# Attention scores from rounded high and low parts instead of plain fp32 matmuls

## The chip, the core and the metric

One core of a Trainium2 chip. The time is that of the device for one launch, in microseconds (us), the median of the runs shown; smaller is better.

## The reference

One layer of a diffusion backbone on 128 context tokens and 1024 latent tokens, D_MODEL 1024: a SwiGLU half step, then attention beside a recurrent block (RG-LRU), then a second SwiGLU half step. The change touches the differential attention:

```python
s = jnp.einsum('bqhmd,bkhmd->bhmqk', qi, k) * scale      # 4 heads h, 2 maps m, d = 64
p = jax.nn.softmax(s, axis=-1)
pd = p[:, :, 0] - lam * p[:, :, 1]
return jnp.einsum('bhqk,bkhv->bqhv', pd.astype(v.dtype), v)
```

Context queries see the 128 context keys. Latent queries see 1024 latent keys, rotated by RoPE as the queries are, and 128 cached keys: 1152 in all. Everything is float32.

## The kernel before

Activations stand transposed, features on the partitions: x holds queries of head hd in tile hd (map 0 on partitions 0 to 63, map 1 on 64 to 127) and its keys in tile hd + 4. The FFN and the projections use products in two rounded parts: each operand is split into a high part (type fp32r, a rounding copy on ScalarE) and a low part (operand less high part, on VectorE), and three fp32r matmuls add high by high, high by low and low by high (`three`, lines 715 to 719). The attention scores don't: `scores` (line 1034) takes x and the cached keys kc as plain fp32, 64 rows per map, each map in its half of the array (`tile_position`). The trace has two records for each plain fp32 matmul and one for each fp32r matmul.

A unit u is one head (u // 9) and one tile of 128 queries (u % 9); unit 0 of a head is the context tile with 128 keys, the eight others are full units with 1152 keys. There are 36. PSUM has banks 0 to 2 for the scores of map 0, 3 to 5 for map 1, bank 6 for transposes and bank 7 for outputs, one copy of each. The four engines run written-out orders, one pass per u:

- TensorE: `scores(u)` (each map waits on e_done until its exponential of unit u-1 has been taken), then for unit u-2 three groups of three transposes through bank 6 (`group`), with the value products of unit u-3 between them (`values`, line 1061).
- VectorE (line 2323): the negated row maximum of each map (`maxima`), the copy of the middle group of transposes of unit u-2 (`p_copy`), the difference of the two maps of unit u-1 (three instructions), and the output of unit u-3.
- ScalarE (line 1593): copy of the first group of transposes, the exponentials of both maps with their sums, copy of the last group, and the squares of unit u-4's output.
- POOL: nothing until the norm of the outputs near the end. SP: all DMA.

Ahead of the loop, VectorE rotates the eight q and k tiles (`rope`), gates the recurrent block (`rg_gated`, line 2249) when xg is no longer needed, and computes lambda; SP then loads vc, ident, kc and dl over xg (N_ACST). ScalarE evicts the v products (`v_evac`), 15 ahead of the loop and three in it behind unit 1, where TensorE makes the last three v tiles (`v_last`). SP loads the first two tiles of w_out (lines 677 and 678) there; they are used at units 32 and later. When a head's last scores are done, SP reloads its two x tiles, which were spilled before.

## Time and profile before

| | |
|---|---|
| three runs | 2266.53, 2268.42, 2269.19 us; median 2268.42 |
| the profiled execution | span 2266.8 us from first to last instruction; the page gives no time around it |
| TensorE matmuls busy | 2191.9 us, 97% |
| VectorE, ScalarE, POOL busy | 1552.2 (68%), 815.4 (36%), 20.1 us (1%) |
| mean granted TensorE clock | 0.992 |

Busy time counts instructions that compute; a matmul's record is longer than the distance to the next, since they are pipelined, so the records of one group can add up to more than the time that they take. In the chain of what ended last each step goes back to what released it.

### The profile page before, as it was taken

What the parts mean: (1) busy time and instruction counts of PE and PEld (TensorE: products, weight loads), DVE (VectorE), ACT (ScalarE), POOL (GpSimd) and SP (SyncE); (2) the same over time, 40 slices, a digit from 0 to 9 for tenths busy, and PEclk for the clock granted to TensorE, in tenths of its full rate; (3) what the DMA queues carried; (4) which work ended last, traced back from release to release, by engine and by line L of the source; (5) the groups of instructions that cost most, each with busy time, mean ns of one, the idle gap of its engine ahead of it and who ended that gap; (6) DMA issues with size and microseconds to landing.
All of it is one profiled execution on the core that took longest, in us unless ns stands there. A gap on an engine that the chain in (4) does not pass through costs nothing.

```text
span 2266.8 us, 33980 instructions
## 1 busy us (share of the span) xinstructions
PE 2191.9 (97%) x13144; PEld 2105.5 (93%) x13144; DVE 1552.2 (68%) x2607; ACT 815.4 (36%) x1458; POOL 20.1 (1%) x31
## 2 busy tenths in 40 slices
PE   5999999999999999999999999999999999999997
PEld 4989999999999999889977779899999999999996
DVE  6977777778888776666668874686454556756556
ACT  5532222334111144654255662353232323421122
POOL 0000000000000000000000030000000000000000
PEclk9999999999999999999999999999999999999998
DMA  7433333344624304010110011132212123431312
GB/s 290 133 105 135 103 126 111 113 138 131 213 78 158 126 27 151 19 47 28 32 49 22 22 40 38 56 114 68 78 59 86 58 87 101 159 120 52 109 41 84
DMA packets 82292, 210.10 MB, mean 93 GB/s; under 512 B 9856, under 2 KB 36352, under 8 KB 82176
## 3 DMA queue, kind: packets, MB, share of 16 engines
q1 hardware_dynamic: 82176, 208.52, 27.4%
q8 instruction: 78, 1.28, 0.2%
q14 instruction: 38, 0.31, 0.0%
HBM read 172.56 MB, written 35.92 MB: 92 GB/s over the span
## 4 chain that ended last, share of the span: by engine, by line
PE 88%; DVE 7%; ACT 2%; DMA 1%; issue 1%; SPq 0%; DVEq 0%; ACTq 0%
PE ps L717 15%; PE ps L719 15%; PE ps L718 15%; PE ps L792 9%; PE ps L793 9%; PE ps L794 9%; PE ps L972 6%; PE ps L1043 4%; PE ps L1072 2%; PE ps L1058 1%; PE ps L954 1%; DVE sb_nmx L2286 1%; DVE sb_hL L1752 1%; DVE sb_tmp L1761 1%; PE ps L741 1%
## 5 line engine op out<-in xcount | busy, mean ns | idle before, releaser
L717 PE MATMUL ps<-sb_hH,sb_wH 128*128 128x384 f32 x1664 | 562.7, 338 | 10.2 <-DVE sb_hL L1752 4.7
L719 PE MATMUL ps<-sb_hH,sb_wL 128*128 128x384 f32 x1664 | 557.4, 335 | 0.0
L718 PE MATMUL ps<-sb_hL,sb_wH 128*128 128x384 f32 x1664 | 557.3, 335 | 0.0
L717 PEld LDWEIGHTS ps<-sb_hH,sb_wH 128*128 128x128 f32 x1664 | 313.4, 188 | 17.5 <-DVE sb_hL L1752 6.0
L718 PEld LDWEIGHTS ps<-sb_hL,sb_wH 128*128 128x128 f32 x1664 | 313.4, 188 | 1.1
L719 PEld LDWEIGHTS ps<-sb_hH,sb_wL 128*128 128x128 f32 x1664 | 313.4, 188 | 0.0
L2062 DVE SCALAR_TENSOR_TENSOR sb_x<-ps,sb_mod,sb_x 128x384 f32<-128x384 f32 (+2 forms) x384 | 186.2, 513 | 172.6 <-PE ps L719 167.2
L792 PE MATMUL ps<-sb_hH,sb_wH 128*128 128x384 f32 x704 | 236.1, 335 | 4.1 <-DVE sb_tmp L1922 3.9
L793 PE MATMUL ps<-sb_hL,sb_wH 128*128 128x384 f32 x704 | 235.9, 335 | 0.0
L794 PE MATMUL ps<-sb_hH,sb_wL 128*128 128x384 f32 x704 | 235.8, 335 | 0.0
L1226 ACT ACTIVATE sb_wH<-sb_wide 128x512 fp32r<-128x512 f32 x176 | 110.8, 633 | 229.1 <-DVE sb_wide L1806 224.0
L1215 ACT ACTIVATE sb_wH<-sb_raw 128x512 fp32r<-128x512 f32 x212 | 129.7, 627 | 172.3 <-PE ps L719 69.2
L1360 ACT ACTIVATE sb_wH<-sb_raw 128x512 fp32r<-128x512 f32 (+1 forms) x96 | 56.8, 596 | 371.0 <-PE ps L719 363.4
L1788 DVE TENSOR_TENSOR sb_wL<-sb_raw,sb_wH 128x512 fp32r<-128x512 f32 x212 | 139.7, 685 | 58.5 <-ACT sb_wH L1215 58.1
L794 PE MATMUL ps<-sb_r2H,sb_wL 128*128 128x384 f32 x528 | 176.4, 334 | 0.0
L792 PE MATMUL ps<-sb_r2H,sb_wH 128*128 128x384 f32 x528 | 176.4, 334 | 0.0
L793 PE MATMUL ps<-sb_r2L,sb_wH 128*128 128x384 f32 x528 | 176.4, 334 | 0.0
L792 PEld LDWEIGHTS ps<-sb_hH,sb_wH 128*128 128x128 f32 x704 | 132.7, 188 | 5.2 <-issue 5.2
L794 PEld LDWEIGHTS ps<-sb_hH,sb_wL 128*128 128x128 f32 x704 | 132.8, 189 | 0.0
L793 PEld LDWEIGHTS ps<-sb_hL,sb_wH 128*128 128x128 f32 x704 | 132.6, 188 | 0.0
L1812 DVE TENSOR_TENSOR sb_wL<-sb_wide,sb_wH 128x512 fp32r<-128x512 f32 x176 | 114.0, 684 | 2.4 <-DVE sb_rq L1863 1.1
L2286 DVE TENSOR_REDUCE sb_nmx<-ps 128x1 f32<-128x1152 f32 (+1 forms) x72 | 85.8, 1233 | 39.3 <-PE ps L1043 39.3
(244 smaller groups left out, 3789.3 us busy)
## 6 DMA issues: line engine op xcount, KB each, us to landing
sb_raw<-in_w_gate SPq DMA_DIRECT2D x56, 512.0 KB, 3.7
sb_raw<-in_w_up SPq DMA_DIRECT2D x56, 512.0 KB, 3.6
sb_raw<-in_w_mod SPq DMA_DIRECT2D x56, 512.0 KB, 3.5
hidden<-sb_tmp SPq DMA_DIRECT2D x132, 192.0 KB, 2.2
sb_hid_raw<-hidden SPq DMA_DIRECT2D x40, 576.0 KB, 6.5
sb_raw<-in_w_dn SPq DMA_DIRECT2D x80, 256.0 KB, 2.7
sb_stage<-in_w_mod SPq DMA_DIRECT2D x4, 2048.0 KB, 15.4
sb_raw<-in_w_in SPq DMA_DIRECT2D x16, 512.0 KB, 3.5
```

The lines of the kernel that those rows point to most:

```text
L717: pe.matmul(o, wH, xH, start=begin, stop=False)
L718: pe.matmul(o, wH, xL, start=False, stop=False)
L719: return pe.matmul(o, wL, xH, start=False, stop=end)
L792: pe.matmul(dst, wH[:, slot, at], opv(0, b, k), start=begin and k == 0, stop=False, skip_group_check=True)
L793: pe.matmul(dst, wH[:, slot, at], opv(1, b, k), start=False, stop=False, skip_group_check=True)
L794: m = pe.matmul(dst, wL[:, slot, at], opv(0, b, k), start=False, stop=k == 3, skip_group_check=True)
L972: m = pe.matmul(dst, (wiH, wiH, wiL)[part][:, f, at], hv((hH, hL, hH)[part], c, k), start=s == 0, stop=s == 3 * KT - 1)
L1215: act.activation(wH[:, o if slot is None else slot], raw_of(o, other), ACT.Copy).then_inc(one_hi[o], 1)
L1226: act.activation(wH[:, at], wide[:, 8 + at], ACT.Copy).then_inc(sum_hi, 1)
L1788: dve.tensor_tensor(wL[:, at], raw_of(o, other), wH[:, at].bitcast(F32), ALU.subtract).then_inc(one_lo[o], 1)
L1812: dve.tensor_tensor(wL[:, at], wide[:, 8 + at], wH[:, at].bitcast(F32), ALU.subtract).then_inc(sum_lo, 1)
L2062: m = dve.scalar_tensor_tensor(x[:, t, b:e], ps[:, DOWN_BANKS[n % 6], b - c * CH:e - c * CH], mod[:, gate + t, cond:cond + 1], x[:, t, b:e ...
```

## The change

Each full unit's scores are now sums of fp32r matmuls. Queries of head hd are rounded (high part) and stand twice on the 128 partitions, for each map by itself (`qstack`, `q_first`). Keys stand as high part on one half of the partitions and low part on the other (`kstack0` to `kstack2`, with the cached keys behind the latent ones). A 128-row matmul so gives high by high plus high by low at once, in three pieces of 384 keys, one for each bank. A third pass of 64 rows per map adds the low part of the queries times the high part of the keys (`low_scores`). Map 0 goes stacked then low, map 1 low then stacked, so that the low passes of both maps stand side by side. Context tiles stay as they were.

The low parts overwrite x in place (`qk_rest`). ScalarE rounds (`qk_high`) and VectorE subtracts (`qk_low`): head 0 ahead of the loop, the others at the units in SPLIT_AT. POOL issues the copies within SBUF that stack them, 12 for each head. The new buffers share space with raw, x, tmp, hL, wiH and xg. The w_out loads move behind the first head's last score.

```diff
@@ -60,9 +60,9 @@
 GROUP0 = [0] + [1 + 3 * t for t in range(9)]
 GROUPS = GROUP0[9]
 UNIT = LAT + 128
-PIECES = ((0, 0, 512), (0, 512, 1024), (1, 0, 512), (0, 1024, UNIT), (1, 512, 1024), (1, 1024, UNIT))
 MIX_ORDERS = ((0, 1, 2, 4, 5, 6, 7, 3), (4, 5, 6, 7, 0, 1, 2, 3), (4, 5, 6, 7, 0, 1, 2, 3))
 MIX_ORDER = MIX_ORDERS[1]
+SPLIT_AT = {1: (1, 0), 3: (1, 1), 5: (2, 0), 7: (2, 1), 11: (3, 0), 13: (3, 1)}
 LAM_INIT = 0.8 - 0.6 * math.exp(0.0)
 KEYS = T + 128
 GRID_W = 64
...
@@ -302,11 +320,27 @@
 
         ssf = ss[:].rearrange("p h t -> p (h t)")
 
-        psf = ps[:].rearrange("p b n -> p (b n)")
         o_first = raw[:, 2:4].rearrange("p a n -> p (a n)")
 
         def unit(u, m):
-            return psf[:, m * 1536:m * 1536 + KEY_TILES[u % QT] * P]
+            return ps[:, 3 * m:3 * m + 3, 0:CH] if u % QT else ps[:, 3 * m, 0:P]
+
+        def by_bank(row):
+
+            return row.rearrange("p (a n) -> p a n", a=3)
+
+        def queries(hd):
+
+            return qstack[:, hd - 1] if hd else q_first[:]
+
+        def keys_of(hd):
+
+            return (kstack0, kstack1, kstack2, kstack0)[hd]
+
+        def tile_hi(hd, is_k):
+
+            return 2 * hd + is_k + 1 + (hd > 0)
+
 
         def probs(u, m):
             return pr[:, u % 3, m, 0:KEY_TILES[u % QT] * P]
@@ -674,13 +708,13 @@
             sp.dma_start(out["v"], v[:, 0]).then_inc(outs, 16)
             sp.wait_ge(m_ev, 6 + 12 + QK * NC)
             sp.dma_start(out["k"].rearrange("h p t -> p h t"), x[:, 4:8, 0:CTX]).then_inc(outs, 16)
-            load_raw(0, used_wo[0], a["w_out"][0])
-            load_raw(1, used_wo[1], a["w_out"][1])
-
             sp.wait_ge(outs, 48)
             sp.wait_ge(spilled, 16 * KT)
             for hd in range(NH):
                 sp.wait_ge(s_ready, (hd + 1) * 2 * QT)
+                if hd == 0:
+                    load_raw(0, used_wo[0], a["w_out"][0])
+                    load_raw(1, used_wo[1], a["w_out"][1])
                 for k in (hd, hd + NH):
                     sp.dma_start(x[:, k], xd[k]).then_inc(xback, 16)
             with sp.Fori(0, 3) as i:
@@ -700,6 +734,41 @@
         @blk.gpsimd
         def _(pool):
 
+            top, bottom = slice(0, DH), slice(DH, P)
+
+            def stack_queries(hd):
+
+                pool.wait_ge(qk_hi, tile_hi(hd, 0))
+                if hd == 0:
+                    for s in range(2):
+                        pool.wait_ge(raw_used[s], used_wo[s] + 1)
+                elif hd == 1:
+                    pool.wait_ge(v_ready, 18)
+                for m, r in ((0, top), (1, bottom)):
+                    for to in (top, bottom):
+                        pool.dma_start(queries(hd)[to, m], qk_split[r]).then_inc(qk_moved, 16)
+
+            def stack_keys(hd):
+
+                pool.wait_ge(qk_hi, tile_hi(hd, 1))
+                if hd:
+                    pool.wait_ge(qk_in, 96 * hd)
+                if hd == 3:
+                    pool.wait_ge(s_ready, 2 * QT)
+                for m, r in ((0, top), (1, bottom)):
+                    pool.dma_start(keys_of(hd)[r, m, 0:LAT], qk_split[r]).then_inc(qk_moved, 16)
+                pool.wait_ge(qk_lo, tile_hi(hd, 1))
+                lows = qk_rest[:, hd + NH, CTX:T]
+                for m, r, to in ((0, top, bottom), (1, bottom, top)):
+                    pool.dma_start(keys_of(hd)[to, m, 0:LAT], lows[r]).then_inc(qk_in, 16)
+                pool.wait_ge(qk_lo, 3)
+                for m, r, to in ((0, top, bottom), (1, bottom, top)):
+                    pool.dma_start(keys_of(hd)[r, m, LAT:UNIT], kcH[r, hd]).then_inc(qk_in, 16)
+                    pool.dma_start(keys_of(hd)[to, m, LAT:UNIT], kcL[r, hd]).then_inc(qk_in, 16)
+
+            for hd in range(NH):
+                stack_queries(hd)
+                stack_keys(hd)
             pool.wait_ge(o_rec, 1)
             for c in range(NC):
                 for hd in range(NH - 1):
@@ -1031,19 +1100,50 @@
                     m = pe.transpose(ps[:, turn_bank(c, hd), k * P:(k + 1) * P], attended(hd, c * 3 + k), ident[:])
                 m.then_inc(ot_ready, 1)
 
-            def scores(u):
-
-                hd, q = u // QT, u % QT
-                for m, b, e in ((0, 0, P), (1, 0, P)) if q == 0 else PIECES:
-                    if b == 0 and 2 * u + m > 1:
+            def context_scores(u):
+
+                hd = u // QT
+                for m in range(2):
+                    if u:
                         pe.wait_ge(e_done, 2 * u + m - 1)
                     r = slice(m * DH, (m + 1) * DH)
-                    at = CTX if q else 0
-                    keys = kc[r, hd] if b == LAT else x[r, hd + NH, at + b:at + e]
-                    mm = pe.matmul(unit(u, m)[:, b:e], x[r, hd, q * P:(q + 1) * P], keys, start=True, stop=True,
-                                   tile_position=(m * DH, 0))
-                    if e == (UNIT if q else P):
-                        mm.then_inc(s_ready, 1)
+                    pe.matmul(unit(u, m), x[r, hd, 0:P], x[r, hd + NH, 0:P], start=True, stop=True,
+                              tile_position=(m * DH, 0)).then_inc(s_ready, 1)
+
+            def stacked_scores(u, m, begin):
+
+                hd, q = u // QT, u % QT
+                for p in range(3):
+                    mm = pe.matmul(ps[:, 3 * m + p, 0:CH], queries(hd)[:, m, (q - 1) * P:q * P],
+                                   keys_of(hd)[:, m, p * CH:(p + 1) * CH], start=begin, stop=not begin)
+                return mm
+
+            def low_scores(u, m, p, begin):
+
+                hd, q = u // QT, u % QT
+                r = slice(m * DH, (m + 1) * DH)
+                return pe.matmul(ps[:, 3 * m + p, 0:CH], qk_rest[r, hd, q * P:(q + 1) * P],
+                                 keys_of(hd)[r, m, p * CH:(p + 1) * CH], start=begin, stop=not begin,
+                                 tile_position=(m * DH, 0))
+
+            def scores(u):
+
+                hd, q = u // QT, u % QT
+                if q == 0:
+                    context_scores(u)
+                    return
+                if q == 1:
+                    pe.wait_ge(qk_lo, tile_hi(hd, 0))
+                    pe.wait_ge(qk_moved, 96 * hd + 96)
+                    pe.wait_ge(qk_in, 96 * hd + 96)
+                pe.wait_ge(e_done, 2 * u - 1)
+                stacked_scores(u, 0, True)
+                pe.wait_ge(e_done, 2 * u)
+                for p in range(3):
+                    mm = low_scores(u, 0, p, False)
+                    low_scores(u, 1, p, True)
+                mm.then_inc(s_ready, 1)
+                stacked_scores(u, 1, False).then_inc(s_ready, 1)
 
             def group(u, g):
 
@@ -1537,7 +1637,20 @@
                 later_evac(i)
                 if i % NC == NC - 1:
                     gelu_of(i // NC - QK)
+            def qk_high(hd, is_k):
+
+                if hd or is_k:
+                    act.wait_ge(qk_moved, 96 * hd + 64 * is_k)
+                    act.wait_ge(qk_lo, tile_hi(hd, is_k) - 1)
+                act.activation(qk_split[:], x[:, hd + NH * is_k, CTX:T], ACT.Copy).then_inc(qk_hi, 1)
+
             for n in range(15):
+                if n == 4:
+                    qk_high(0, 0)
+                elif n == 10:
+                    qk_high(0, 1)
+                    act.wait_ge(acst, N_ACST)
+                    act.activation(kcH[:], kc[:], ACT.Copy).then_inc(qk_hi, 1)
                 if n == 6:
                     act.wait_ge(v_half, 1)
                     cast(wiH[:, 0], 2, used_in[2] + 2)
@@ -1561,8 +1674,8 @@
 
                 if u < TILES:
                     act.wait_ge(mx_ready, 2 * u + m + 1)
-                    act.activation(probs(u, m), unit(u, m), ACT.Exp, bias=nmx[:, u % 2, m:m + 1],
-                                   accum_out=sums[:, u % 3, m:m + 1]).then_inc(e_done, 1)
+                    act.activation(by_bank(probs(u, m)) if u % QT else probs(u, m), unit(u, m), ACT.Exp,
+                                   bias=nmx[:, u % 2, m:m + 1], accum_out=sums[:, u % 3, m:m + 1]).then_inc(e_done, 1)
 
             def out_squares(u):
 
@@ -1597,6 +1710,8 @@
                 if u == 1:
                     for n in range(15, 18):
                         v_evac(n)
+                if u in SPLIT_AT:
+                    qk_high(*SPLIT_AT[u])
                 p_copy(u - 2, 2)
                 if u >= 4:
                     out_squares(u - 4)
@@ -2269,6 +2384,17 @@
             for j in range(1, RGT):
                 rg_gated(j)
 
+            def qk_low(hd, is_k):
+
+                xt = x[:, hd + NH * is_k, CTX:T]
+                dve.wait_ge(qk_hi, tile_hi(hd, is_k))
+                dve.tensor_tensor(qk_rest[:, hd + NH * is_k, CTX:T], xt, qk_split[:].bitcast(F32),
+                                  ALU.subtract).then_inc(qk_lo, 1)
+
+            qk_low(0, 0)
+            qk_low(0, 1)
+            dve.wait_ge(qk_hi, 3)
+            dve.tensor_tensor(kcL[:], kc[:], kcH[:].bitcast(F32), ALU.subtract).then_inc(qk_lo, 1)
             dve.wait_ge(acst, N_ACST)
             for j in range(2):
                 link(dve.tensor_tensor(dl[:, 2 * j], dl[:, 2 * j], dl[:, 2 * j + 1], ALU.mult))
@@ -2283,7 +2409,8 @@
             def maxima(u, m):
 
                 dve.wait_ge(s_ready, 2 * u + m + 1)
-                dve.tensor_reduce(nmx[:, u % 2, m:m + 1], unit(u, m), AX.X, ALU.max, negate=True).then_inc(mx_ready, 1)
+                dve.tensor_reduce(nmx[:, u % 2, m:m + 1], unit(u, m), AX.XY if u % QT else AX.X, ALU.max,
+                                  negate=True).then_inc(mx_ready, 1)
 
             def difference(u):
 
@@ -2329,6 +2456,8 @@
                     difference(u - 1)
                 if u >= 3:
                     output(u - 3)
+                if u - 1 in SPLIT_AT:
+                    qk_low(*SPLIT_AT[u - 1])
                 if u in (TILES - 1, TILES):
                     f = u - TILES + 1
                     lo(wiL[:, f], f, None, wiH[:, f], whi_wo + f + 1)
```

## Rows read from the trace of the kernel before

**Rows 1.** The page, parts 1 and 4: the whole span.
```profile
PE 2191.9 (97%) x13144; PEld 2105.5 (93%) x13144; DVE 1552.2 (68%) x2607; ACT 815.4 (36%) x1458; POOL 20.1 (1%) x31
...
PE 88%; DVE 7%; ACT 2%; DMA 1%; issue 1%; SPq 0%; DVEq 0%; ACTq 0%
```

**Rows 2.** The windows view: busy us (and instructions) of each engine, clock, DMA.
```profile
1131.35:1163.80 32.45, 29.02 (x159) 23.22 (x160) 16.41 (x23) 12.60 (x24) 0.00 (x0) 0.84 0.15 50
1163.80:1187.23 23.43, 23.43 (x158) 17.72 (x157) 20.21 (x29) 14.93 (x33) 0.00 (x0) 1.00 0.09 29
1187.23:1238.20 50.97, 49.17 (x320) 37.10 (x320) 42.04 (x63) 30.93 (x72) 0.00 (x0) 1.00 0.07 24
```

**Rows 3.** The timeline (start us, us), TensorE in one steady full unit.
```profile
1163.80 2.37 PE L1043 MATMUL ps<-sb_x 64*128 64x512 f32 x8
...
1166.32 0.55 PE L1058 MATMUL ps<-sb_ident,sb_pr 128*128 128x128 f32 x3
1166.60 1.20 PEld L1072 LDWEIGHTS ps<-sb_v,sb_pT 128*128 128x128 f32 x10
1166.71 1.28 PE L1072 MATMUL ps<-sb_v,sb_pT 128*128 128x128 f32 x10
...
1169.18 0.55 PE L1058 MATMUL ps<-sb_ident,sb_pr 128*128 128x128 f32 x3
...
1169.66 0.69 PE L1043 MATMUL ps<-sb_x 64*128 64x512 f32 x1
```

**Rows 4.** The timeline of the same unit, VectorE and ScalarE.
```profile
1166.04 2.62 DVE L2286 TENSOR_REDUCE sb_nmx<-ps 128x1 f32<-128x1152 f32 x2 [0.75 <-PE ps L1043]
...
1167.43 1.22 ACT L1564 ACTIVATE sb_pr<-ps,sb_nmx 128x1152 f32<-128x1152 f32 x1
...
1168.58 0.55 DVE L2310 COPY sb_pT<-ps 128x384 f32<-128x384 f32 x1
1168.69 1.22 ACT L1564 ACTIVATE sb_pr<-ps,sb_nmx 128x1152 f32<-128x1152 f32 x1
```

**Rows 5.** The timeline, TensorE: starts of the scores in head 1.
```profile
1191.72 2.09 PE L1043 MATMUL ps<-sb_x 64*128 64x512 f32 x8
...
1197.58 2.38 PE L1043 MATMUL ps<-sb_x 64*128 64x512 f32 x8
...
1202.58 2.38 PE L1043 MATMUL ps<-sb_x 64*128 64x512 f32 x6
...
1208.77 2.28 PE L1043 MATMUL ps<-sb_x 64*128 64x512 f32 x7
```

**Rows 6.** The timeline in the FFN: two fp32r matmuls in a row.
```profile
700.27 0.33 PE L719 MATMUL ps<-sb_hH,sb_wL 128*128 128x384 f32 x1
...
700.44 0.33 PE L717 MATMUL ps<-sb_hH,sb_wH 128*128 128x384 f32 x1
```

**Rows 7.** The timeline around the start of head 0.
```profile
1114.30 3.89 DVE L2253 TENSOR_TENSOR sb_xr<-sb_xr,sb_xg 128x1152 f32<-128x1152 f32 x3
1123.71 0.22 DVE L2274 TENSOR_TENSOR sb_dl<-sb_dl 128x64 f32<-128x64 f32 x1 [5.53 <-DMA sb_dl<-in_dl]
...
1131.35 3.94 PE L1043 MATMUL ps<-sb_x 64*128 64x512 f32 x8 [0.91 <-ACT sb_pr L1564]
...
1146.48 2.62 DVE L2286 TENSOR_REDUCE sb_nmx<-ps 128x1 f32<-128x1152 f32 x2 [7.87 <-PE ps L1043]
...
1149.24 4.19 PE L1043 MATMUL ps<-sb_x 64*128 64x512 f32 x7 [2.43 <-ACT sb_pr L1564]
```

**Rows 8.** The timeline, the line view and the DMA view: prices of the new work.
```profile
1113.15 1.22 DVE L1670 TENSOR_TENSOR sb_wiL<-sb_raw,sb_wiH 128x1024 fp32r<-128x1024 f32 x1 [3.37 <-ACT sb_wiH L1164]
...
L1164 ACT ACTIVATE sb_wiH<-sb_raw x26: 1044/1054/1069, 794.5 to 1435.3; 128x1024 fp32r<-128x1024 f32 x26
...
sb_x<-x_spilled SPq DMA_DIRECT2D x8, 576.0 KB, 4.9
...
sb_kc<-in_kc SPq DMA_DIRECT2D x1, 256.0 KB, 3.5
```

More of the change, by code:

```diff
@@ L133, in build @@
         lnorm = sb("lnorm", [P, 32])
+        with ExitStack() as s:
+            q_first = sb("q_first", [P, 2, LAT], F32R, s)
         raw = sb("raw", [P, SLOTS, 1024])
+        with ExitStack() as s:
+            qk_rest = sb("qk_rest", [P, KT, T], F32R, s)
         x = sb("x", [P, KT, T])
+        with ExitStack() as s:
+            qk_split = sb("qk_split", [P, LAT], F32R, s)
         tmp = sb("tmp", [P, 5, CH])
@@ L147, in build @@
             hid_raw = sb("hid_raw", [P, NC * KT * CH], F32, s)
+        with ExitStack() as s:
+            qstack = sb("qstack", [P, NH - 1, 2, LAT], F32R, s)
+            kstack1 = sb("kstack1", [P, 2, UNIT], F32R, s)
         hL = sb("hL", [P, NC * KT * CH], F32R, acts)
@@ L165, in build @@
         mid = ExitStack()
+        with ExitStack() as s:
+            kstack2 = sb("kstack2", [P, 2, UNIT], F32R, s)
         wiH = sb("wiH", [P, 2, 1024], F32R, mid)
@@ L193, in build @@
             nlam = sb("nlam", [P, 1], F32, s)
+            kstack0 = sb("kstack0", [P, 2, UNIT], F32R, s)
+            kcH = sb("kcH", [P, NH, P], F32R, s)
+            kcL = sb("kcL", [P, NH, P], F32R, s)
         mid.close()
@@ L279, in build @@
         roped = sem("roped")
+        qk_hi = sem("qk_hi")
+        qk_lo = sem("qk_lo")
+        qk_moved = sem("qk_moved")
+        qk_in = sem("qk_in")
         s_ready = sem("s_ready")
```

4 lines of the change are left out of this document (2 added, 2 removed).

## The prediction

> **What bounds the kernel now.** I read the page first [rows 1]: TensorE is busy for 97% of the span and holds 88% of the chain that ended last, so the kernel is bound by TensorE as a whole. The change touches one stage only, the attention units, and an average over the span says nothing about that stage. So I cut the stage with the windows view [rows 2], one window from head start to head start. A head takes 50.97 us; between 1163.80 and 1187.23 four full units run in 23.43 us, 5.86 us each, with TensorE busy in all of it, VectorE in 20.21 us (5.05 us per unit) and ScalarE in 14.93 us (3.73 per unit). TensorE is the fullest, but VectorE is only 0.81 us per unit behind it: that is the most that a cheaper TensorE can give.
>
> The timeline of one such unit [rows 3] shows how TensorE spends 5.86 us: the scores from 1163.80 to the first transposes at 1166.32 (2.52 us), then transposes and value products for 3.34 us up to the next scores at 1169.66. Two small readings there matter later. Three transposes followed by value products take 0.39 us (1166.32 to 1166.71); three transposes followed by scores take 0.48 us (1169.18 to 1169.66): going from the whole array to its two halves costs about 0.09 us. And ten weight loads of 128 columns take 1.20 us, 0.12 us each.
>
> The other engines of the same unit [rows 4] show a second loop as tight as the first. The maximum of map 0 starts 2.24 us after the scores (1163.80 to 1166.04); both maxima and the copy of the middle transposes follow in 2.54 + 0.55 us; the last transposes wait for that copy (1169.18), and the next scores come 0.48 us later. 2.24 + 2.54 + 0.55 + 0.05 + 0.48 = 5.86 us. Making the matmuls cheaper pays only because this loop gets shorter as well.
>
> At the start of a head the steps differ [rows 5]: 4.49 us (a short unit first, from 1187.23), then 5.86, 5.00 and 6.19 to 1208.77. What is left of the head's 50.97 us are 29.43 for five steps, 5.89 each. The step of 5.00 us is a wait: 2.24 from scores to maximum, 1.39 to the exponential, 1.22 for it and 0.15 back to TensorE.
>
> **The change, part by part.** *Scores.* Now a full unit issues, per map, two 512-column and one 128-column plain fp32 matmul on 64 rows, the two maps side by side. Afterwards it issues three stacked 384-column fp32r matmuls on 128 rows per map (six), and three 64-row ones per map (six, in pairs). The 384-column fp32r matmul stands in the FFN rows [rows 6]: one every 0.173 us, each record 0.33 us long. Six stacked: 1.04 us. A 64-row fp32r pair isn't in the trace. Below, it costs one pitch if the two halves overlap fully, 3 x 0.173 = 0.52 us; above, two pitches, 1.04 us. I take 0.24 us a pair, two weight loads at 0.12 [rows 3], since the maps do overlap now (eight 512-column records in 2.37 us, while 128-column ones alone take 0.12 each, or 0.48 per 512 columns, 3.8 us for eight): 0.72 us. The scores now go into the halves once and leave them once, between transposes and scores; afterwards they do both inside the scores. I count 0.09 us each way, 0.18, and take 0.09 off the transposes before. Bounds for the two passages: nothing, and 0.32 us (two times a record's length less its pitch, 0.33 - 0.173 [rows 6]). Sum: 1.04 + 0.72 + 0.18 = 1.94 us for 2.52 + 0.09: 0.67 us less per full unit (0.21 with both upper bounds, 1.05 with both lower ones, which VectorE's 5.05 us cuts to 0.81).
>
> The page "TensorEngine Tiling (Array Packing)" of the Trainium skill, section "Tiling Modes", says that changing the tiling mode drains the engine. The passage of 0.09 us in rows 3 is less than the 0.16 us by which a record outlasts its pitch, so this trace doesn't show a full drain in front of the scores. By the page the two passages would be worth 0.32 us instead of 0.18 and the whole gain about 4 us less.
>
> *Does the second loop shrink too?* Map 0 is complete after its three stacked and two and a half pairs: 0.52 + 0.09 + 0.6, then the end of a record (0.16 more) and the hand-over (0.05): 1.4 us instead of 2.24. The loop becomes 1.4 + 2.54 + 0.55 + 0.05 + 0.39 = 4.93 us. But the low pass of both maps now waits for the exponential of map 1 of the unit before. By rows 4 that ends 1.39 + 1.26 + 1.22 + 0.1 = 3.97 us after the first maximum starts; from the low pass to the next maximum are 0.9 us: 4.87 us. So after the change TensorE needs 5.86 - 0.67 = 5.19, VectorE 5.05, the loops 4.93 and 4.87. With everything this close I expect 5.26 us a step, 0.60 less than now.
>
> *Per head.* The short unit keeps its plain matmuls: 0. The step of 5.00 hangs on score to maximum to exponential and loses 0.8. The step of 6.19 now starts with a wait for map 1's exponential (it starts right after map 0's, 1.3 us earlier than map 1's is done, while the stacked part covers only 0.5): it loses 0.2. The six others lose 0.6 each: 4.6 us a head, 13.8 for heads 1 to 3.
> Head 0 runs partly at half clock (mean 0.84 in the first window of rows 2) and with gaps. Its unit 1 needs 3.94 us for the eight records that take 2.37 at full clock [rows 3, 7], so some 4.2 us for 2.52; nine pitches of twice 0.173 are 3.1, and passages: 1.0 less. Unit 2 loses 0.6, the way from its scores to its exponential 0.8; unit 3 (seven such records in 4.19 us, so about 4.8 us in all) comes down to 3.1 plus passages and loses 1.3. Units 4 to 8 lose 2.8 together. Head 0: 6.5. Sum of gains 20.3 us.
>
> *Splitting.* Each 128x1024 tile now costs ScalarE a rounding copy (1.05 us) and VectorE a subtraction (1.22 us) [rows 8]. Two tiles come before the loop, six inside it (units 1, 3, 5, 7, 11, 13; the subtraction one unit later, behind the output of unit u-3 and ahead of the next maxima, for which the exponentials, and through them the scores, wait). VectorE has about 0.2 us of slack in a 5.26 us step, so a subtraction lengthens it by 1.0. The first falls into the gaps of head 0's first units (the wait of 7.87 us in rows 7 is ahead of unit 2's maxima) and is free; the second I take as half free. 0.5 + 4 x 1.05 = 4.7, say 5 us (2 if the slack is larger, 7.3 if nothing hides). ScalarE has 1.5 us of slack per step: the copies cost nothing, except that they push back the last copy of transposed probabilities by 1.05 us, which the next unit's transposes await; I count 0.5 us in all (0 to 3).
>
> *The start of head 0.* ScalarE's first copy goes between two v evictions, for which TensorE waits only five products later: nothing. VectorE is free at 1118.2 (three gated products from 1114.30 [rows 7]), so: subtraction of q to 1119.4, ScalarE's copy of k to 1120.6, its subtraction to 1121.9. The cached keys come with the constants, whose last one lands at 1123.7 [rows 7]; copy and subtraction of 512 columns (0.63 + 0.65): 1125.1. Then POOL issues four small copies (32 KB each) behind eight larger ones. The trace has no copy within SBUF and none issued by POOL; the nearest rows are 256 KB in 3.5 us and 576 KB in 4.9 us [rows 8]. Unit 1 could start at 1131.35, 6.2 us later. If the four overlap they land by 1129: no cost. If each takes 3.5 us after the one before, 1139: 8 us. I take 1.5, being nearer to overlap. ScalarE's wait for the constants holds back two v evictions, for which TensorE waits only in front of unit 0, some 5 us after they are done. The kernel's w_out loads move from head 0 behind its last score, some 150 us ahead of their use, still ahead of the x reloads in SP's queue: nothing.
>
> The page "DMA: Bandwidth & Descriptors" of the Trainium skill, section "Anatomy of one DMA — SWDGE (gpsimd) path", gives about 2.0 us plus the bytes at 436 GB/s for a POOL-issued copy. No row here shows one; by that estimate the small copies land near 1128 and the start costs nothing, a total 1.5 us better.
>
> *The rest.* The maximum and the exponential read the same 1152 columns as three pieces of 384: same cost (in one piece 2.62 us for two maxima and 1.22 us for an exponential [rows 4]). Copies for heads 1 to 3 are issued many units ahead of their use; DMA is at 7 to 9% of its time there [rows 2]. What follows attention starts when it ends, and is TensorE again.
>
> Sum: 20.3 - 5 - 0.5 - 1.5 = 13.3 us. The profiled span is 2266.8 us, 1.6 below the median of 2268.42 and within the runs (2266.53 to 2269.19); 2266.8 - 13.3 = 2253.5 for the span, 2255.1 for the median.
>
> **Rivals.** (1) *VectorE becomes the bound*: pairs overlap fully and passages are free. Steps of 5.05 plus little, 0.75 less each: 32 x 0.15 = 4.8 us more gain, the start free: 2248. For it: the two maps overlap now. Against it: four loops within 0.3 us of each other.
> (2) *The pairs don't overlap and each passage drains*: 0.21 us per full unit, 6.7 us, and some 2 more for the half-clock part, against 7 us of new work: 2267, no change. For it: K of 64 in fp32r is nowhere in the trace.
> (3) *Slower*: inside the mode change every 64-row matmul runs at its record's length, one after another, weight load in the open: 6 x 0.33 + 1.04 + 0.18 = 3.2 us against 2.61, 0.59 us more in each of 32 units, 19 us, plus 7 for splits and start: 2294. This side begins where the scores take over 2.4 us, because the new work of 7 us is 0.22 us per unit. Against it: the plain 64-row matmuls of rows 3 don't do it.
> (4) *Start-up stall*: POOL's copies land one by one, unit 1 starts 8 us late, the clock falls, another 2 us: 2263.
>
> **How the numbers follow.** Forecast (2250 to 2260) 0.50; rival 1 0.16, rival 2 0.14, rival 3 0.09, rival 4 0.11. The range of 8 in 10 takes in rivals 1, 4 and most of 2: 2245 to 2267. A measurement of this kernel tells about 0.2%, 4.5 us, from no change: faster means under 2263.9. Forecast, rival 1 and most of rival 4 lie there: 0.76. Within: rival 2 and the rest, 0.14. Slower: 0.10.
>
> **What would show it.** Starts of scores in steady steps 5.2 to 5.3 us apart; scores to first transposes 1.9 us; a head of about 46 us plus the splits (two in head 0's second half and two in head 1's first); TensorE no longer busy in all of the window, VectorE over 95%. Pairs: the two 64-row records start together or 0.12 apart. Wrong if the scores stay above 2.3 us, if the maximum starts more than 1.6 us after the scores, if VectorE waits for TensorE as long as now (0.75 us), or if unit 1 of head 0 starts over 3 us late.

## The result and the profile after

The changed kernel takes 2249.53 us (median of four runs, 2246.93 to 2250.85) where the kernel before, on the same chip, takes 2268.63 (2266.53 to 2269.19): 0.9917 of the time, with an interval of 0.9903 to 0.9931, or 19.1 us less. The forecast was 2255.1, a gain of 13.3. The profiled span is 2248.9 us (before 2266.8).

The page of the kernel after, parts 1, 3 and 4, answers to [rows 1]:

```profile
PE 2168.4 (96%) x13144; PEld 2105.0 (94%) x13144; DVE 1560.1 (69%) x2616; ACT 823.1 (37%) x1467; POOL 44.6 (2%) x79
...
q0 software_dynamic: 3840, 8.92, 1.8%
...
PE 84%; DVE 10%; ACT 2%; DMA 2%; issue 1%; SPq 1%; DVEq 0%; ACTq 0%
```

VectorE's share of the chain that ended last rose from 7% to 10%, TensorE's fell from 88% to 84%, which fits a stage that has changed its bound. VectorE gained nine instructions (eight subtractions of q and k tiles, one of the cached keys), and a queue of copies issued by POOL is new.

The windows view of the kernel after, with the columns of [rows 2]: the last four full units of head 0, head 1, head 2, and three steady steps of head 2.

```profile
1163.28:1185.85 22.57, 20.64 (x159) 17.77 (x158) 22.29 (x31) 16.84 (x35) 6.11 (x12) 1.00 0.43 93
1185.85:1232.60 46.75, 42.54 (x320) 36.62 (x319) 44.70 (x66) 32.73 (x74) 9.17 (x18) 1.00 0.49 126
1232.60:1277.10 44.50, 42.26 (x320) 36.63 (x319) 41.30 (x63) 30.60 (x72) 0.00 (x0) 1.00 0.08 30
1256.78:1271.89 15.11, 15.11 (x120) 13.38 (x119) 14.89 (x21) 10.97 (x25) 0.00 (x0) 1.00 0.00 1
```

Head 2 has no split left in it and takes 44.50 us instead of 50.97. Its steady step is 15.11 / 3 = 5.04 us instead of 5.86, and VectorE is busy in 14.89 of the 15.11 us. Before, it was busy in 20.21 of 23.43 [rows 2]. TensorE shows 15.11 of 15.11 although it is not the fullest engine any more, as the experiments show: a matmul's record outlasts the distance to the next, and the records cover pauses as short as those here (0.07 us a step). Its busy share can't tell here whether it is the bound.

The timeline of one such unit, TensorE and VectorE, answers to [rows 3, 4]:

```profile
1261.82 0.77 PE L1117 MATMUL ps<-sb_kstack,sb_qstack 128*128 128x384 f32 x3
...
1262.53 0.78 PE L1125 MATMUL ps<-sb_kstack,sb_qk_rest 64*128 64x384 f32 x6
...
1263.24 0.80 PE L1117 MATMUL ps<-sb_kstack,sb_qstack 128*128 128x384 f32 x3
1263.42 2.61 DVE L2412 TENSOR_REDUCE sb_nmx<-ps 128x1 f32<-128x1152 f32 x2
...
1263.88 0.49 PE L1158 MATMUL ps<-sb_ident,sb_pr 128*128 128x128 f32 x3
...
1265.95 0.55 DVE L2437 COPY sb_pT<-ps 128x384 f32<-128x384 f32 x1
...
1266.56 0.55 PE L1158 MATMUL ps<-sb_ident,sb_pr 128*128 128x128 f32 x3
...
1266.86 0.77 PE L1117 MATMUL ps<-sb_kstack,sb_qstack 128*128 128x384 f32 x3
```

The scores take 2.06 us (1261.82 to 1263.88; before 2.52). The maxima have no bracket behind them: VectorE comes to them from other work, 1.60 us after the scores began. Before, it stood 0.75 us waiting for them. The transposes at 1266.56 start 0.06 us after the copy ends (1265.95 + 0.55), as they did before.

Where the 17.9 us between the two profiled spans come from, by the start of unit 0's maxima and the start of the last full unit's: the stretch ahead of unit 0 is 3.1 us longer (1133.59 against 1130.51), the attention loop 21.1 shorter (185.91 against 207.05), what follows 0.2 longer (929.4 against 929.24). The first of these isn't the change: in a second profile of the same kernel (below) the stretch ends at 1130.76, and in the first the delay is there long before the changed lines run (ScalarE's same rounding copy of a weight tile starts at 598.15 us there, at 595.37 in the second profile and at 595.14 in the kernel before).

### The profile page after: what moved, and what is told of

Read it like the earlier page. It is cut to its first block, busy times and chain, and to the rows that moved or that the text cites. A ratio compares the mean times of both kernels' runs of the same rounds, so it can differ in the third digit from the quotient of the medians.

```text
span 2248.9 us, 34067 instructions
## 1 busy us (share of the span) xinstructions
PE 2168.4 (96%) x13144; PEld 2105.0 (94%) x13144; DVE 1560.1 (69%) x2616; ACT 823.1 (37%) x1467; POOL 44.6 (2%) x79
## 4 chain that ended last, share of the span: by engine, by line
PE 84%; DVE 10%; ACT 2%; DMA 2%; issue 1%; SPq 1%; DVEq 0%; ACTq 0%
PE ps L786 15%; PE ps L788 15%; PE ps L787 15%; PE ps L861 9%; PE ps L863 9%; PE ps L862 9%; PE ps L1041 7%; DVE sb_nmx L2412 3%; PE ps L1023 1%; DVE sb_pr L2422 1%; DMA sb_stage<-in_w_mod 1%; PE ps L1172 1%; PE ps L1158 1%; PE ps L1125 1%; ACT sb_pr L1677 1%
## 5 line engine op out<-in xcount | busy, mean ns | idle before, releaser
L1999 DVE TENSOR_TENSOR sb_tmp<-ps,sb_tmp 128x384 f32<-128x384 f32 x32 | 17.9, 558 | 120.1 <-PE ps L863 119.0
```

## The experiments

Each ratio is to runs of the kernel before on the same chip. "Step" is the distance from one full unit's maxima to the next in the steady part of a head.

**The changed kernel again.** No edit.

> The changed kernel once more, as the measure for its neighbours on this chip: 2249.5 us, 19 below the kernel before.

0.9903 [0.9886, 0.9919], 2246.71 us. Step 5.04; heads 0 to 2, by the starts of their scores, 54.49, 46.76, 44.48 us, where the first profile of this kernel has 52.83, 46.75, 44.50 and the kernel before 57.28, 50.97, 50.97; loop 187.53. Heads 1 and 2 repeat to 0.02 us; head 0 differs by 1.7 us between the two profiles of one kernel, so what an edit does to head 0 can't be read from one profile. The granted clock differs there: from unit 0's scores to unit 2's it is 1.00 in the first profile (12.18 us) and 0.77 in the second (15.10 us), from there to unit 5's 0.72 (18.08 us) and 0.90 (16.83 us). These two stretches hold the 1.7 us; what is left of the head takes 22.57 and 22.56 us.

### What the low pass costs

**Low pass issued twice.** Its sum of scores is another one.

```diff
...
                 for p in range(3):
+                    low_scores(u, 0, p, False, False)
+                    low_scores(u, 1, p, True, False)
+                for p in range(3):
                     mm = low_scores(u, 0, p, False)
-                    low_scores(u, 1, p, True)
+                    low_scores(u, 1, p, False, False)
```

> The changed kernel with every low pass issued twice (the low part counts double in the scores): 0.52 us more of TensorE per full unit if the two maps run side by side, 1.04 if they don't. TensorE stands at about 4.97 us of 5.04, so theory V and rival T both give steps of 5.5 and 32 x 0.45 = 14 us more if the pairs overlap, 30 us if not. If something hides it (rival: TensorE has real slack), under 5 us.

0.9966 [0.9955, 0.9977], 2260.94 us; step 5.50. The timeline, TensorE and VectorE:

```profile
1261.13 1.31 PE L1125 MATMUL ps<-sb_kstack,sb_qk_rest 64*128 64x384 f32 x12
...
1262.38 0.80 PE L1117 MATMUL ps<-sb_kstack,sb_qstack 128*128 128x384 f32 x3
1262.48 2.62 DVE L2415 TENSOR_REDUCE sb_nmx<-ps 128x1 f32<-128x1152 f32 x2 [0.36 <-PE ps L1125]
```

Twelve 64-row matmuls take 1.25 us (1261.13 to 1262.38) where six take 0.71 (1262.53 to 1263.24): three more pairs, 0.54 us, 0.18 each, which is one pitch of 0.173 [rows 6]. The two halves overlap fully. VectorE now waits 0.36 us: TensorE has become the bound. The run is 14.2 us slower than the changed kernel beside it (2246.71), as expected for pairs that overlap.

**Low pass map by map**: three matmuls of map 0, then three of map 1, instead of by turns.

```diff
                 for p in range(3):
                     mm = low_scores(u, 0, p, False)
+                mm.then_inc(s_ready, 1)
+                for p in range(3):
                     low_scores(u, 1, p, True)
-                mm.then_inc(s_ready, 1)
```

> The changed kernel with the low pass issued three for map 0, then three for map 1, instead of in turns. If the halves run side by side only when neighbours in the queue are of different halves: one pair overlaps at the seam, 0.35 us more per unit, 10 us slower. If the order doesn't matter: same.

0.9908 [0.9891, 0.9924], 2246.61 us; step 5.04, no change. Six matmuls in this order take 0.72 us too (1263.44 to 1264.16): the engine overlaps the halves whether their matmuls alternate or stand three and three.

**Low pass on the whole array.** Its 128 rows take in rows that don't belong there; the scores are others.

```diff
-                return pe.matmul(ps[:, 3 * m + p, 0:CH], qk_rest[r, hd, q * P:(q + 1) * P],
-                                 keys_of(hd)[r, m, p * CH:(p + 1) * CH], start=begin, stop=not begin,
-                                 tile_position=(m * DH, 0))
+                return pe.matmul(ps[:, 3 * m + p, 0:CH], qk_rest[:, hd, q * P:(q + 1) * P],
+                                 keys_of(hd)[:, m, p * CH:(p + 1) * CH], start=begin, stop=not begin)
```

> The changed kernel with the low pass as six 128-row matmuls over the whole array, one after another (the rows of the other half are added too, so the scores are others): no passage into halves and back. Six at 0.173 = 1.04 us instead of 0.52 for the pairs plus two passages. The trace shows 0.70 and 0.72 us from one pass of three to the next where three pitches are 0.52, so the passages cost 0.18 to 0.20 each: scores of 2.1 to 2.2 us instead of 2.06, steps within 0.1, 0 to 4 us slower. If the passages cost 0.09 each as I had counted: 0.34 us more per unit, 9 us slower.

0.9936 [0.9919, 0.9952], 2253.51 us; step 5.19. The timeline:

```profile
1261.47 0.77 PE L1117 MATMUL ps<-sb_kstack,sb_qstack 128*128 128x384 f32 x3
...
1262.08 1.28 PE L1125 MATMUL ps<-sb_kstack,sb_qk_rest 128*128 128x384 f32 x6
...
1263.21 2.62 DVE L2411 TENSOR_REDUCE sb_nmx<-ps 128x1 f32<-128x1152 f32 x2
...
1263.71 0.49 PE L1157 MATMUL ps<-sb_ident,sb_pr 128*128 128x128 f32 x3
```

The scores take 2.24 us (1261.47 to 1263.71) with three pitches more, 0.52 us, and no passage; in the kernel after they take 2.06. So the passages cost at least 2.06 - (2.24 - 0.52) = 0.34 us together. From the stacked to the low part there are 0.71 us with the halves (1261.82 to 1262.53) and 0.61 here (1261.47 to 1262.08), 0.10 of the 0.34. From the low part to the transposes there are 1.35 us with the halves, 0.31 over six pitches, and 1.63 here, 0.07 over nine; the difference of 0.24 holds the way back and what the way in leaves behind it. In both kernels the low part must wait for ScalarE's exponential of map 1 of the unit before, which ends 0.19 us ahead of it in the kernel after and 0.08 here. If the 0.07 come from that wait, and the kernel after has it hidden behind its passage, the passages cost 0.41; that part is argued, not shown. The page "TensorEngine Tiling (Array Packing)" of the Trainium skill, section "Tiling Modes", says that a change of mode drains the engine; that fits, since a record outlasts its pitch by 0.16 us. Pairs save three pitches and pay two passages: 0.52 less 0.34 to 0.41, only 0.1 to 0.2 us of TensorE's time per unit.

The step is longer by 0.15 us, and by these rows a loop sets it: map 0's maximum starts 1.13 us after the low part (1262.08 to 1263.21; 0.89 in the kernel after), that maximum and the next lead to the exponential of map 1, and the next low part starts as soon as that has ended. The run takes 6.9 us more than the one before, on the same chip. That is above the 0 to 4 us expected for passages of 0.18 to 0.20: 32 x 0.15 are 4.8, and 1.3 lie in the stretch after attention, which the edit doesn't touch.

### What sets the step

**The low pass left out.** The product of the queries' low part is missing from the scores.

```diff
...
-                stacked_scores(u, 0, True)
+                stacked_scores(u, 0, True, True).then_inc(s_ready, 1)
                 pe.wait_ge(e_done, 2 * u)
-                for p in range(3):
-                    mm = low_scores(u, 0, p, False)
-                    low_scores(u, 1, p, True)
-                mm.then_inc(s_ready, 1)
-                stacked_scores(u, 1, False).then_inc(s_ready, 1)
+                stacked_scores(u, 1, True, True).then_inc(s_ready, 1)
```

> The changed kernel without the low pass (the low part of the queries is left out of the scores): TensorE does 0.7 us less per full unit. Theory V (VectorE, 5.05 us a unit, sets the step of 5.04): steady steps stay at 5.04, only the steps at head starts that wait for an exponential get shorter, 0.7 us each; 2 to 5 us faster than the changed kernel in all. Rival T (TensorE still sets the step): 0.7 us less in 28 steps, 20 us faster. Rival L (the way from the scores to the first maximum sets it, and would be 0.7 us shorter): the same 20 us.

0.9892 [0.9875, 0.9908], 2243.96 us; step 5.03, where the kernel after has 5.04. TensorE has some 0.9 us less to do in each unit (three pitches and the passages), and nothing comes of it:

```profile
1262.59 2.61 DVE L2408 TENSOR_REDUCE sb_nmx<-ps 128x1 f32<-128x1152 f32 x2
...
1265.72 0.55 PE L1154 MATMUL ps<-sb_ident,sb_pr 128*128 128x128 f32 x3 [0.33 <-DVE sb_pT L2433]
...
1267.62 2.61 DVE L2408 TENSOR_REDUCE sb_nmx<-ps 128x1 f32<-128x1152 f32 x2
```

Now TensorE waits for VectorE's copy. This rules out TensorE as the bound of the steady step, and with it the way from the scores to the first maximum, which is shorter by the low pass too. In all the run is 2.75 us faster than the changed kernel beside it. Head 2 takes 44.12 us for 44.48: its third step falls from 4.28 to 3.57 us, but its fifth grows from 5.04 to 5.68. There the granted clock is 0.50, the lower of its two levels (1246 to 1248), after a stretch in which TensorE was busy in only 2.68 of 4.00 and 1.04 of 2.00 us (1240 to 1246); the kernel after holds 1.00 all through heads 1 and 2. The fall is seen behind the pauses; that they caused it isn't shown.

**The output on ScalarE.** `output(u - 3)`, 0.35 us of VectorE per unit, moves to ScalarE behind its last copy.

```diff
+            def act_output(u):
+                act.wait_ge(pd_ready, u + 1)
+                act.wait_ge(o_ready, u + 1)
...
+                act.activation(attended(u // QT, u % QT), ps[:, 7, 0:P], ACT.Copy,
+                               scale=rec[:, u % 6, 0:1]).then_inc(o_done, 1)
...
-                if u >= 3:
-                    output(u - 3)
```

> The changed kernel with the output scaling of unit u-3 (0.35 us, a pitch of 0.26) on ScalarE instead of VectorE. Theory V with TensorE at 4.97 right behind: steps of 4.97 to 5.0, 1 to 3 us faster; in the split steps and at head starts, where VectorE alone sets it, 0.26 each more. Rival: ScalarE's later exponentials cost more than VectorE gains: slower.

0.9911 [0.9894, 0.9927], 2247.20 us; step 4.97. TensorE and VectorE:

```profile
1262.45 2.62 DVE L2423 TENSOR_REDUCE sb_nmx<-ps 128x1 f32<-128x1152 f32 x2
...
1262.98 0.49 PE L1158 MATMUL ps<-sb_ident,sb_pr 128*128 128x128 f32 x3
1263.31 1.28 PE L1172 MATMUL ps<-sb_v,sb_pT 128*128 128x128 f32 x10
...
1265.42 0.39 PE L1172 MATMUL ps<-sb_vc,sb_pT 128*128 128x128 f32 x2
1265.64 0.50 PE L1158 MATMUL ps<-sb_ident,sb_pr 128*128 128x128 f32 x3
1265.89 0.77 PE L1117 MATMUL ps<-sb_kstack,sb_qstack 128*128 128x384 f32 x3
...
1267.42 2.62 DVE L2423 TENSOR_REDUCE sb_nmx<-ps 128x1 f32<-128x1152 f32 x2
```

Nothing pushes TensorE back here: 2.06 us of scores and 2.91 of transposes and value products (1262.98 to 1265.89) are 4.97. So TensorE's own need is 4.97 us, 0.07 below VectorE's, and the move of 0.26 us (the pitch of that instruction) buys 0.07 per step. With the split steps (5.92 us for 6.17) that makes some 3 us in all, and the attention loop is 2.7 us shorter than the shorter of the kernel after's two (183.2 us for 185.9 and 187.5); but the stretch after attention is 1.9 us longer, for a reason that stays open (see the end of the next section), and the median can't be told from the kernel after.

**Both**: output on ScalarE and no low pass (the same product is missing).

> As the run before, and without the low pass (the low part of the queries is left out of the scores). Theory V: with TensorE 0.7 us cheaper only VectorE counts, 5.05 - 0.26 = 4.8 us a step, so it gains 0.24 x 28 = 7 us on the run that only leaves out the low pass. If something else holds the step at 5.04 (rival L or ScalarE), no more than 2 us.

0.9866 [0.9849, 0.9882], 2238.10 us, 5.9 below the run that only leaves out the low pass (7 expected). The maxima, 4.77 and 4.78 us apart:

```profile
1252.97 2.62 DVE L2419 TENSOR_REDUCE sb_nmx<-ps 128x1 f32<-128x1152 f32 x2
1257.74 2.62 DVE L2419 TENSOR_REDUCE sb_nmx<-ps 128x1 f32<-128x1152 f32 x2
1262.52 1.35 DVE L2419 TENSOR_REDUCE sb_nmx<-ps 128x1 f32<-128x1152 f32 x1
```

5.04 - 0.26 = 4.78: with TensorE out of the way, VectorE gives back all that is taken from it. Relief of TensorE alone gives 0.01, of VectorE alone 0.07, of both 0.26: two bounds of nearly the same height.

**The same move in the kernel before.**

> The kernel before with the output scaling on ScalarE. Before, TensorE (5.86 us a step) and the loop over the maxima set the step and VectorE had 0.8 us to spare, so its relief buys nothing there: within 2 us of the kernel before. If VectorE had set the step already then: 0.26 x 28 = 7 us faster.

1.0006 [0.9997, 1.0016], 2270.15 us; head 2 takes 50.94 us for 50.97. In the kernel before VectorE's load doesn't matter, which shows that it became a bound only through the change.

**Both maps' stacked parts first, then the low pass.** TensorE has the same work; map 0 is done later.

```diff
...
                 stacked_scores(u, 0, True)
                 pe.wait_ge(e_done, 2 * u)
+                stacked_scores(u, 1, True)
                 for p in range(3):
                     mm = low_scores(u, 0, p, False)
-                    low_scores(u, 1, p, True)
+                    m1 = low_scores(u, 1, p, False)
                 mm.then_inc(s_ready, 1)
-                stacked_scores(u, 1, False).then_inc(s_ready, 1)
+                m1.then_inc(s_ready, 1)
```

> The changed kernel with the stacked passes of both maps first and the low pairs behind them: TensorE does the same matmuls with the same two passages (in and out of halves), but map 0 is done about 0.7 us later and the stacked pass of map 1 waits for the exponential. Rival L's loop, now 4.93 us, becomes 5.6: if it counts, steps of 5.5 to 5.7, 32 x 0.55 = 18 us slower. Theory V without a tight loop beside it: steps stay at 5.04, within 3 us.

0.9991 [0.9981, 1.0001], 2266.14 us; step 5.57. Nearly the whole gain is gone without one matmul more: 19.4 us over the changed kernel beside it, 18 expected if the loop counts. The timeline:

```profile
1261.37 1.37 PE L1117 MATMUL ps<-sb_kstack,sb_qstack 128*128 128x384 f32 x6
...
1262.68 0.78 PE L1125 MATMUL ps<-sb_kstack,sb_qk_rest 64*128 64x384 f32 x6
...
1263.50 2.62 DVE L2413 TENSOR_REDUCE sb_nmx<-ps 128x1 f32<-128x1152 f32 x2 [0.44 <-PE ps L1125]
...
1266.64 0.55 PE L1159 MATMUL ps<-sb_ident,sb_pr 128*128 128x128 f32 x3 [0.37 <-DVE sb_pT L2438]
```

From the scores to the maximum are 2.13 us instead of 1.60, and now each engine waits for the other (0.44 and 0.37 us). That is the loop of the prediction: 2.13 + 2.54 + 0.60 + 0.30 = 5.57. Finishing map 0 early is worth 0.53 us a step; the cheaper matmuls without it gain 0.29 in a steady step (5.86 to 5.57), and less than 1 us in all of head 2 (50.31 for 50.97).

### The splits

**Subtractions of heads 1 to 3 on POOL.**

```diff
+            def pool_low(hd, is_k):
+                if hd:
+                    xt = x[:, hd + NH * is_k, CTX:T]
+                    pool.tensor_tensor(qk_rest[:, hd + NH * is_k, CTX:T], xt, qk_split[:].bitcast(F32),
+                                       ALU.subtract).then_inc(qk_lo, 1)
...
-                if u - 1 in SPLIT_AT:
-                    qk_low(*SPLIT_AT[u - 1])
```

> The changed kernel with the six subtractions for heads 1 to 3 on POOL instead of VectorE, behind POOL's own copies. Theory V: each subtraction on VectorE stretches its step by 1.1 us, the first hidden: 5 to 5.6 us faster than the changed kernel, head 1 at 44.5 us instead of 46.75. Rival: the splitting costs through ScalarE's rounding copy (1.05 us ahead of its last copy of transposes), which stays: under 1 us.

0.9914 [0.9897, 0.9931], 2248.51 us: no gain over the kernel after that can be told. The four steps with a visible split (6.15, 6.17, 6.17, 6.17 us in the kernel after) now take 5.28, 6.25, 6.44 and 5.27: two are nearly free, two are longer than they were, and head 1 takes 46.37 us where 44.5 were expected. The two free ones keep ScalarE's rounding copy, so that copy (the rival) isn't what costs. In the timeline of the second, a small VectorE instruction before and during POOL's subtraction:

```profile
1166.38 0.22 DVE L2429 SCALAR_TENSOR_TENSOR sb_coef<-sb_sums,sb_nlam,sb_rec 128x1 f32<-128x1 f32 x1
...
1170.41 2.40 POOL L743 TENSOR_TENSOR sb_qk_rest<-sb_x,sb_qk_split 128x1024 fp32r<-128x1024 f32 x1
1171.41 1.43 DVE L2429 SCALAR_TENSOR_TENSOR sb_coef<-sb_sums,sb_nlam,sb_rec 128x1 f32<-128x1 f32 x1
```

It ends with POOL's (1172.84 and 1172.81) and takes 1.43 us instead of 0.22: the 1.22 us taken off VectorE come back as its wait. In all six cases this instruction, which reads only SBUF, ends within 0.04 us of POOL's; in the two cheap steps POOL starts right behind two copies instead of four, and the wait is 0.2 to 0.3 us. VectorE's copy from PSUM and its reciprocal, inside the same POOL subtraction, keep their 0.55 and 0.15 us. The page "SBUF — State Buffer" of the Trainium skill, section "SBUF: two separate sides", says that a GpSimd instruction and a VectorE one with two SBUF inputs exclude each other for a whole instruction, and this row agrees.

**Both moves** (output on ScalarE, subtractions on POOL).

> The changed kernel with the output scaling on ScalarE and the subtractions for heads 1 to 3 on POOL. If both work as expected they add up: 6 to 9 us faster than the changed kernel, 2241 to 2244.

0.9907 [0.9891, 0.9924], 2247.73 us: again the kernel after, within what can be told. None of the versions that compute all of the scores beats it clearly.

### The moved loads

**The kernel before with its two w_out loads moved.**

```diff
-            load_raw(0, used_wo[0], a["w_out"][0])
-            load_raw(1, used_wo[1], a["w_out"][1])
...
+                if hd == 0:
+                    load_raw(0, used_wo[0], a["w_out"][0])
+                    load_raw(1, used_wo[1], a["w_out"][1])
```

> The kernel before with only the loads of w_out moved behind head 0's last score. My count: nothing, within 2 us of the kernel before. Rival (the two 512 KB loads disturb head 0's first units): part of the 19 us, 2 to 4 us faster than the kernel before.

1.0000 [0.9990, 1.0009], 2267.96 us: the move neither costs nor gains anything, as forecast.

## Why the prediction was right, and where its size was off

Faster came true, and 2249.5 lies in the range of 2245 to 2267, just below the 2250 to 2260 that had half of the chance; the gain was 19.1 us instead of 13.3. The mechanism held in this: the cheaper scores shorten TensorE's work and the second loop together, and VectorE stands close behind as the limit. The engine that it named as the new bound was the wrong one. Step by step, sizes by the profiled executions:

**The step: 5.26 forecast, 5.04 measured. This is the term that was mis-sized.** The prediction took TensorE's need as 5.86 - 0.67 = 5.19 us, above VectorE's 5.05, and so TensorE as the bound. But 5.86 us were not TensorE's need. Two lines of the kernel before that the prediction passed over, TensorE's matmuls and its weight loads:

```profile
1168.82 0.39 PE L1072 MATMUL ps<-sb_vc,sb_pT 128*128 128x128 f32 x2
...
1169.18 0.31 PEld L1058 LDWEIGHTS ps<-sb_ident,sb_pr 128*128 128x128 f32 x3 [0.16 <-DVE sb_pT L2310]
```

The last value products to the last transposes: 0.36 us there, 0.22 with the output on ScalarE (1265.42 to 1265.64), where nothing waits. The 3.34 us that the prediction carried over whole held 0.19 us of waiting for the copy (0.14 ahead of the transposes, and 0.05 in them, which take 0.30 us to the next scores in the kernel after, where they wait too, and 0.25 here), 0.18 for the passage into the halves (0.48 in [rows 3] against 0.30) and 0.06 for the passage out (0.39 against 0.33). It took off 0.09 where 0.43 went: 2.91 us is what is left. So TensorE's need before was 5.86 - 0.19 = 5.67 us, and the 5.86 were the second loop, which had no slack in it: that loop, not TensorE, set the step before. Against that the scores take 2.06 us instead of 1.94: the pairs 0.52 instead of 0.72, the six stacked 1.04 as forecast, and 0.50 for the passages and what follows them instead of 0.18. That this sum came out only 0.12 off is luck: pairs 0.20 too dear, passages 0.32 too cheap. The passage was read too low because three transposes ahead of value products (0.39) were taken as the undisturbed case, and those had just come out of the halves themselves. TensorE's need is 4.97, and VectorE's 5.04 sets the step: rival 1's bound, with pairs as it assumed them, but passages at twice the forecast's price where it had them free.

**The second loop: 4.93 forecast.** It was rightly counted: with the output on ScalarE, from scores to maximum 1.53 (1265.89 to 1267.42; 1.4 forecast), maxima 2.54, copy 0.55, and 0.35 to the next scores are 4.97, of which 0.05 are no part of the loop (the copy ends at 1265.54, its hand-over takes 0.05, the transposes come at 1265.64): 4.92. That it must shrink, or nothing is won, is what the run with both stacked parts first showed (5.57).

**Per head: 4.6 forecast, 6.5 measured in head 2.** The scores of head 2 start 4.31, 5.02, 4.28, 5.54, 5.03, 5.04, 5.04, 5.03 and 5.21 us apart. The first, the short unit, loses 0.18 (0 forecast), the step of 5.00 comes down to 4.28 (0.72 for 0.8), the one of 6.19 to 5.54 (0.65 for 0.2): the exponential of map 1 is awaited there, but less long. The steady ones lose 0.82 instead of 0.6: six of them are 1.3 of the 1.9 us that the forecast missed per head, and the 6.19 step is most of the rest.

**The splits: 5 us forecast, 4.5 measured.** VectorE's subtraction and the starts of the scores around it:

```profile
1216.19 0.77 PE L1117 MATMUL ps<-sb_kstack,sb_qstack 128*128 128x384 f32 x3
...
1217.79 1.22 DVE L2391 TENSOR_TENSOR sb_qk_rest<-sb_x,sb_qk_split 128x1024 fp32r<-128x1024 f32 x1
...
1222.36 0.77 PE L1117 MATMUL ps<-sb_kstack,sb_qstack 128*128 128x384 f32 x3
```

That step takes 6.17 us instead of 5.04, 1.13 more. Four of the six do so (the steps from 1163.28, 1174.47, 1204.98 and 1216.19), those in units 2 and 8 are covered: 4 x 1.13 = 4.5. The forecast had the first free, the second (unit 4) half free and the other four in full; the second cost all, and the one in unit 8, ahead of a short unit, nothing. ScalarE's copies cost nothing that shows; 0.5 was forecast.

**The start of head 0: 1.5 us forecast, 0.1 measured.** The timeline there, and the DMA view (KB, median us to landing):

```profile
1130.98 0.53 POOL L767 DMA_DIRECT2D sb_kstack<-sb_kcL  x1
...
1133.02 0.49 PE L1110 MATMUL ps<-sb_x 64*128 64x128 f32 x4 [0.92 <-ACT sb_v L1582]
...
1134.51 0.76 PE L1117 MATMUL ps<-sb_kstack,sb_q_first 128*128 128x384 f32 x3 [1.00 <-ACT sb_pr L1677]
...
sb_kstack<-sb_qk_rest POOLq DMA_DIRECT2D x8, 256.0 KB, 4.1
...
sb_kstack<-sb_kcL POOLq DMA_DIRECT2D x8, 32.0 KB, 2.8
```

Unit 1 follows unit 0 by 1.49 us (1.40 before, 1129.95 to 1131.35), and what it waits for is the exponential, not the copies. The medians of the DMA view are over all four heads. The small copies of head 0 landed faster: the four issued from 1129.47 to 1130.98 took 1.8 us each, so the last was there at 1132.75, 1.8 us ahead of unit 1's scores. That is overlap, as taken, and rival 4 is out. Unit 1 starts 3.16 us later than before by the clock of the profile (1134.51 for 1131.35), which by its letter is the prediction's last sign of being wrong; but those 3 us are the ones that were there at 598 us already. By the page "DMA: Bandwidth & Descriptors" of the Trainium skill, section "Anatomy of one DMA — SWDGE (gpsimd) path", the start was free, which came true; its 2.0 us plus bytes would land 32 KB in 2.1 us and 256 KB in 2.6, and the medians here are 2.8 to 3.0 and 4.1 to 4.3 (the quickest 1.8 and 2.9).

**Sum.** With the splits added back the heads gain 6.8, 6.5, 6.5 and 6.0 us: 57.28 - 52.83 + 2.3 + 0.1 in head 0, 50.97 - 46.75 + 2.3 in head 1, 50.97 - 44.50 in head 2, and for head 3 what is left of the loop's 21.1 plus 4.5 plus 0.1. Together 25.7, where the forecast had 6.5 and three times 4.6, 20.3. Nearly all of the difference, 5.2 us, is in heads 1 to 3, about two thirds of it in the steady steps. In the second profile head 0 gains 5.2 instead of 6.8; its forecast was built from half-clock rows and can't be judged closer than that. 25.7 less 4.5 and 0.1 is 21.1 in one profile and 19.5 in the other; the medians say 19.1.

**Rivals.** The second (no overlap) and the third (slower, one after another) are refuted by the 0.18 us that a pair costs. The first had the right bound, and 2248 is close to 2249.5; but it took the passages as free, and they cost 0.34 to 0.41 us. That this didn't show is because VectorE, not TensorE, sets the step.

**Signs.** Seen as named: VectorE over 95% (14.89 of 15.11), the two records of a pair together (they start within 0.01 us), the splits in the four places. Missed with the size: steps of 5.2 to 5.3 us (5.04), scores of 1.9 (2.06), a head of 46 (44.50). Missed as a sign: TensorE no longer busy all the time (15.11 of 15.11). The maximum starts 1.60 us after the scores, at the edge of what was to count as wrong, because VectorE was still at other work, not because TensorE was late.

Left open: why the granted clock falls in head 0 at another place in each profile, which moves that head by 1 to 2 us (52.83 and 54.49 us in the kernel after; 57.28 before and 56.25 with the w_out loads moved), and a difference of 2 us in the stretch after attention (931.2 us in three profiles, 930.2 and 930.7 in two, 929.2 to 929.7 in the others), which follows no edit: the output on ScalarE has it and so have POOL's subtractions, but both together have not.

## What to carry over

When a cheaper operation is priced from the steady step of the engine that looks fullest, take the step apart first: what it waits for, and which passages go with the operation, must be taken off with it. Count each engine's need and each loop through two engines by itself; the next bound is the highest of them, and relief of one alone is worth no more than its distance to the next. Where two engines hand data round, finish the part that the other waits for first: the order of the same matmuls was worth 0.53 us of a 0.82 us gain per step. And take a busy share of 100% made of overlapping records for what it is: it hides short waits, so the bound has to be found by relieving one engine at a time, and then both.

## What the runs showed of the hardware

- Two 64-row fp32r matmuls of 384 columns on the two halves cost 0.18 us together, as much as one 128-row one (0.173), in turns or three and three.
- Going from the whole array to the halves and back costs 0.34 to 0.41 us (scores of 2.06 us with the halves, 2.24 without them and with three pitches more).
- A POOL subtraction of 128x1024 takes 2.40 us (VectorE 1.22), and a VectorE instruction of 0.22 us (scalar_tensor_tensor, all inputs in SBUF) that falls into it takes 1.43, ending with it; a copy from PSUM and a reciprocal inside it keep their time.
- With the low pass left out TensorE had more pauses, and the granted clock fell to 0.50 once in head 2 (1246 to 1248), which made one step 5.68 us instead of 5.04; in the kernel after it stays at 1.00 in heads 1 and 2.
- A copy within SBUF issued by POOL takes 0.5 us of POOL to issue, and lands 2.8 to 3.0 us after issue for 32 KB and 4.1 to 4.3 for 256 KB (medians; the quickest take 1.8 and 2.9).
